# A three-layer kernel: NSA compression with the sequence stationary, and a first norm computed by token

## The reference, cut to what matters

```python
def rms_norm(x, g):
    y = x * rsqrt(mean(x * x, axis=-1, keepdims=True) + 1e-6)
    return y * g

def compress(t, pe, w1, w2):                 # t: B, S, G=4, DH=64; blocks of 32 tokens, stride 16: nc = 31
    pieces = t.reshape(B, S // 16, 16, G, DH)
    blocks = concatenate([pieces[:, i:i + nc] for i in range(2)], axis=2)
    blocks = blocks + pe[None, None, :, None, :]
    flat = blocks.transpose(0, 3, 1, 2, 4).reshape(B, G, nc, 32 * DH)
    return silu(flat @ w1) @ w2              # w1: 2048 x 256, w2: 256 x 64

# layer 1
h = rms_norm(x, pre_norm[0])
q, k, v, glr, z = split(h @ w_in)            # glr: the 16 columns of a low-rank gate
gk = log_sigmoid(glr @ w_gk_up + b_gk) / 16
# layer 2
kc, vc = rope(keys for compression), values for compression
kcmp, vcmp = compress(kc, pe_k, ck_w1, ck_w2), compress(vc, pe_v, cv_w1, cv_w2)
```

## Time and profile before

| | |
|---|---|
| median of three runs | 1395.79 us |
| the profiled execution | 1399.46 us, span 1397.7 us |
| granted TensorE clock over the span | 0.966 of full speed |
| PE busy | 1318.9 us, 94% |
| VectorE busy | 653.3 us, 47% |
| ScalarE busy | 575.2 us, 41% |
| GpSimd busy | 442.8 us, 32% |

### The profile page before, as it was taken

The page is one execution under the profiler, slowest core; times in us unless marked ns, Lnnn a source line. Parts: engine busy times, 40 slices in busy tenths (PEclk is TensorE's granted clock), DMA queues, the critical chain, the costliest instruction groups (busy, mean ns, idle before and its releaser), DMA issues.

```text
span 1397.7 us, 18116 instructions
## 1 busy us (share of the span) xinstructions
PE 1318.9 (94%) x7220; PEld 1027.4 (74%) x7220; DVE 653.3 (47%) x1005; ACT 575.2 (41%) x973; POOL 442.8 (32%) x216
## 2 busy tenths in 40 slices
PE   5999998978799999999988899999999999999997
PEld 2689876846598776656676588787877888888885
DVE  5343135787871654678852513333333283102533
ACT  4244323442333225678864443444444411434332
POOL 4244411442346221110013442222222264444440
PEclk8899999989899999999999999999999999999999
DMA  5222201533456420210002132222222132333211
GB/s 173 70 91 90 91 31 33 178 103 117 137 169 121 84 60 9 61 31 2 2 6 85 37 93 82 60 61 61 61 61 61 31 120 91 91 106 104 90 61 61
DMA packets 129627, 107.49 MB, mean 77 GB/s; under 512 B 36098, under 2 KB 127360, under 8 KB 129552
## 3 DMA queue, kind: packets, MB, share of 16 engines
q1 hardware_dynamic: 129552, 106.44, 26.2%
HBM read 104.33 MB, written 2.10 MB: 76 GB/s over the span
## 4 chain that ended last, share of the span: by engine, by line
PE 87%; DVE 9%; ACT 2%; issue 1%; DMA 1%; SPq 0%; POOL 0%; DVEq 0%; ACTq 0%
PE banks L1021 46%; PE banks L1012 8%; PE banks L988 4%; PE banks L1476 3%; PE banks L1333 3%; PE banks L1367 2%; PE banks L1352 2%; PE banks L1441 2%; PE banks L1222 2%; PE banks L1390 2%; PE banks L1490 1%; DVE act_lo L1566 1%; DVE y_t L1689 1%; PE banks L1204 1%; DVE ada_sum L1663 1%; PE banks L1336 1%
## 5 line engine op out<-in xcount | busy, mean ns | idle before, releaser
L504 POOL TENSOR_TENSOR w_lo<-raw,w_hi 128x1024 fp32r<-128x1024 f32 x170 | 418.1, 2481 | 893.8 <-ACT w_hi L584 893.7
L1021 PE MATMUL banks<-act_hi,w_hi 128*128 128x512 f32 x848 | 336.8, 397 | 5.1 <-DVEq L1728 5.1
L1021 PE MATMUL banks<-act_lo,w_hi 128*128 128x512 f32 x848 | 332.2, 392 | 0.0
L1021 PE MATMUL banks<-act_hi,w_lo 128*128 128x512 f32 x848 | 332.1, 392 | 0.0
L584 ACT ACTIVATE w_hi<-raw 128x1024 fp32r<-128x1024 f32 x170 | 170.1, 1051 | 129.8 <-PE banks L1021 92.2
L1021 PEld LDWEIGHTS banks<-act_hi,w_hi 128*128 128x128 f32 x848 | 160.5, 189 | 41.8 <-DVEq L1728 5.6
L1021 PEld LDWEIGHTS banks<-act_hi,w_lo 128*128 128x128 f32 x848 | 160.5, 189 | 34.1 <-issue 1.4
L1021 PEld LDWEIGHTS banks<-act_lo,w_hi 128*128 128x128 f32 x848 | 160.3, 189 | 34.0
L1012 PE MATMUL banks<-w_hi,act_hi 128*128 128x256 f32 x320 | 91.6, 286 | 0.0
L1012 PE MATMUL banks<-w_hi,act_lo 128*128 128x256 f32 x320 | 91.3, 285 | 0.0
L1012 PE MATMUL banks<-w_lo,act_hi 128*128 128x256 f32 x320 | 91.2, 285 | 0.0
(11 more groups left out here) (324 smaller groups left out, 2194.7 us busy)
## 6 DMA issues: line engine op xcount, KB each, us to landing
raw<-w_in SPq DMA_DIRECT2D x32, 1024.0 KB, 5.7
raw<-gla_w_in SPq DMA_DIRECT2D x13, 1024.0 KB, 5.3
ada_raw<-w_ada SPq DMA_DIRECT2D x8, 1024.0 KB, 5.6
raw<-nsa_w_in SPq DMA_DIRECT2D x32, 256.0 KB, 4.5
raw<-nsa_w_in SPq DMA_DIRECT2D x7, 1024.0 KB, 5.5
raw<-gla_w_out SPq DMA_DIRECT2D x4, 1024.0 KB, 5.1
ada_first<-w_ada SPq DMA_DIRECT2D x4, 1024.0 KB, 7.9
raw<-nsa_w_out SPq DMA_DIRECT2D x16, 256.0 KB, 4.5
```

The lines of the kernel that those rows point to most:

```text
L504: pool.tensor_tensor(w_lo[:, u, k], raw[:, u, k], w_hi[:, u, k].bitcast(F32), ALU.subtract).then_inc(lo_done, 1)
L1021: mm = pe.matmul(b[:], w[:, u, k, m * P:(m + 1) * P], x[:, k, :], start=(k == 0 and n == 0), stop=(k == KT - 1 and n == 2))
```

## The change

In the start, ACT squares x as it landed, by token, each 128 x 512 half of a token tile with its sum over the row (`tok_squares`), and PE makes the sum for all partitions with eight products of a broadcast column and the identity. DVE takes both parts of chunk 0 and the low part of chunk 1 from ACT and POOL. PE interleaves the tiles: three products of chunk 0, then the four of chunk 1 that need no `w_lo`; the eight tiles' `w_lo` products of chunk 1 follow. The gate product moves between the halves of chunk 2.

In the compression, `kv_hi` and `kv_lo` are laid out by half of the block (`part`), group, block and position pair, and are the stationary operand (128 group-block columns, elements 32 bytes apart); the weights move, 256 columns. There is one loop over the 8 tiles, with `between` behind it. The 32nd block of the last group, unused otherwise, holds the positional vectors. ACT copies the result to `hid_raw` (tokens' blocks on the partitions), and PE turns it with `spread`, the identity with a last row of ones added, which also adds the last row, the bias, to all others. ACT then takes the SiLU without a bias. This turning product stands inside chunk 23 for the keys and behind chunk 27 for the values.

```diff
@@ the start: GpSimd
-            split_range(0, C_KC + 1)
+            pool.wait_ge(lo_done, 2 * C_Q + 2)
+            split_range(C_Q + 1, C_KC + 1)
@@ the start: VectorE
+            def first_low(u, part):
+                k = slice(KT // 2 * part, KT // 2 * (part + 1))
+                dve.tensor_tensor(w_lo[:, u, k], raw[:, u, k], w_hi[:, u, k].bitcast(F32), ALU.subtract).then_inc(lo_done, 1)
+            dve.wait_ge(raw_landed[0], 16)
+            for part in range(2):
+                k = slice(KT // 2 * part, KT // 2 * (part + 1))
+                link(dve.tensor_copy(w_hi[:, 0, k], raw[:, 0, k]))
+            dve.sem_inc(hi_done, 2)
+            first_low(0, 0)
             inverse_root(0)
             split_act(0, lambda k: dve.scalar_tensor_tensor(tmp[:, k % 2], xT[:, k], vcol("pre0", k), rstd[:],
-                                                            ALU.mult, ALU.mult))
+                                                            ALU.mult, ALU.mult), after_first=lambda: first_low(0, 1))
+            dve.wait_ge(hi_done, 2 * C_Q + 2)
+            for part in range(2):
+                first_low(C_Q, part)
@@ the start: ScalarE
+            ln_and_exp()
+            for half in range(2):
+                act.wait_ge(x_landed[half], 16)
+                for t in range(TT):
+                    act.activation(qk[:, TT * half + t], x_tok[:, t, half * S:(half + 1) * S], ACT.Square,
+                                   accum_out=tok_squares[:, half, t:t + 1]).then_inc(sq_ready, 1)
             act.wait_ge(consts_ready, 1)
-            norm_front(0)
-            split_high(0, 0, 0, first=True)
             root(0)
-            split_high(1, 0, 1, first=True)
+            split_high(C_Q, 0, C_Q, first=True)
             high_parts(0)
@@ the start: TensorE
-            mean_square(0, ring_squares(0))
+            for half in range(2):
+                for t in range(TT):
+                    pe.wait_ge(sq_ready, TT * half + t + 1)
+                    pe.matmul(bank[4][:, t * P:(t + 1) * P], tok_squares[:, half, t:t + 1].broadcast_to([P, P]), ident[:],
+                              start=(half == 0 and t == 0), stop=(half == 1), skip_group_check=True).then_inc(sq_used, 1)
...
+                if k % (KT // 2) == 0:
+                    pe.wait_ge(hi_done, 2 * C_Q + 2 * k // KT + 1)
+                for m in range(2):
+                    for x in (act_hi, act_lo):
+                        pe.matmul(bank[2 + m][:], w_hi[:, 1, k, m * P:(m + 1) * P], x[:, k, :],
+                                  start=(k == 0 and x is act_hi), stop=False)
+            for k in range(KT):
+                weights_ready(C_Q, k)
+                for m in range(2):
+                    mm = pe.matmul(bank[2 + m][:], w_lo[:, 1, k, m * P:(m + 1) * P], act_hi[:, k, :],
+                                   start=False, stop=(k == KT - 1))
...
+            product(C_Q + 1, (C_Q + 1) // 2, (C_Q + 1) % 2, between=low_rank_up)
@@ the compression: TensorE
-                for m in range(2):
-                    for k in range(KT):
-                        at = 2 * (KT * part + k)
-                        if m == 0:
-                            weights_ready(c, k)
-                        for n, (w, x) in enumerate(((w_hi, kv_hi), (w_lo, kv_hi), (w_hi, kv_lo))):
-                            mm = pe.matmul(bank[6 + m][:, 0:(NG + 1) * NCP].rearrange("p (g c) -> p g c", c=NCP),
-                                           w[:, u, k, m * P:(m + 1) * P],
-                                           x[:, :, at:at + CS * (NCP - 1) + 1:CS],
...
-                    if m == 0 and between is not None:
-                        between()
+                for k in range(KT):
+                    weights_ready(c, k)
+                    for n, (x, w) in enumerate(((kv_hi, w_hi), (kv_hi, w_lo), (kv_lo, w_hi))):
+                        mm = pe.matmul(bank[6][:, 0:CW], x[:, part, :, :, k].rearrange("p g c -> p (g c)"), w[:, u, k, :],
+                                       start=(part == 0 and k == 0 and n == 0), stop=(part == 1 and k == KT - 1 and n == 2))
+                if between is not None:
+                    between()
                 mm.then_inc(bank_full[2 * u + 1], 1)
...
+            def turn_hidden(i):
+                pe.wait_ge(hid_raw_ready, i + 1)
+                for m in range(2):
+                    mm = pe.matmul(bank[7][:, m * P:(m + 1) * P], hid_raw[:, m * P:(m + 1) * P], spread[:], start=True, stop=True)
+                mm.then_inc(hid_turned, 1)
...
-            product(C_VS, C_VS // 2, C_VS % 2, by_tokens=True)
+            product(C_VS, C_VS // 2, C_VS % 2, by_tokens=True, between=lambda: turn_hidden(0))
@@ the compression: ScalarE and VectorE
+        kv_hi = sb("kv_hi", [P, 2, NG, NCP, CS // 2], F32R)
+        def kv_even(part):
+            return kv_full[:, :, CS * part:CS * part + S:2]
...
-                act.activation(kv_hi[:, 0:NG], kv_full[:], ACT.Copy)
-                act.activation(kv_hi[:, NG, 0:CB:2], pe_t[:, i], ACT.Copy).then_inc(kv_hi_done, 1)
+                for part in range(2):
+                    last = act.activation(kv_hi[:, part].rearrange("p g c k -> p g (c k)"), kv_even(part), ACT.Copy)
+                link(last)
+                act.activation(kv_hi[:, :, NG - 1, NCP - 1, :], pe_halves(i), ACT.Copy).then_inc(kv_hi_done, 1)
+            def hidden_raw(i):
+                c = (C_CK, C_CV)[i] + 1
+                act.wait_ge(bank_full[2 * (c % 2) + 1], c // 2 + 1)
+                act.activation(hid_raw[:], bank[6][:, 0:CW], ACT.Copy).then_inc(hid_raw_ready, 1)
             def hidden(i):
-                act.wait_ge(hid_bias_ready, i + 1)
+                act.wait_ge(hid_turned, i + 1)
...
-            hidden_bias(0)
...
-            hidden_bias(1)
```

More of the change, by code:

```diff
@@ L542, in _ @@
             pool.tensor_copy(maskb[:], wide_zero)
-            pool.memset(kv_hi[:, NG].bitcast(F32), 0.0)
-            link(pool.memset(kv_lo[:, NG].bitcast(F32), 0.0))
+            link(pool.affine_select(out=spread[:], in_=ones[:], compare_op=ALU.is_ge, fill=0.0, base=1 - P,
+                                    pattern=[[0, P]], channel_multiplier=1))
+            link(pool.tensor_tensor(spread[:], spread[:], ident[:], ALU.add))
             pool.sem_inc(consts2_ready, 1)
@@ L781, in _ @@
                 untaken(c)
+            hidden_raw(1)
+            untaken(C_GL)
             hidden(1)
-            untaken(C_GL)
             u = C_GL % 2
@@ L1086, in _, with low_rank_up @@
                                    start=(k == 0 and n == 0), stop=(k == KT - 1 and n == 2))
-            mm.then_inc(bank_full[1], 1)
-            pe.sem_inc(bank_full[0], 1)
-            stream(C_Q, 1)
-            pe.wait_ge(bank_free[1], 1)
-            pe.wait_ge(up_landed, 16)
-            pe.wait_ge(rstd_ready, 1)
-            for h in range(GH):
-                pe.matmul(bank[4 + h][:], w_up[:, h * P:(h + 1) * P], glr_t[:], start=True, stop=True).then_inc(up_full, 1)
-            stream(C_Q + 1, 1)
+                if k == KT - 1:
+                    mm.then_inc(bank_full[1], 1)
+                    pe.sem_inc(bank_full[0], 1)
+                if k % (KT // 2) == 0:
[9 more added lines that the diff above has]
+                                   start=False, stop=(k == KT - 1))
+                    if k == KT - 1:
+                        mm.then_inc(bank_full[2 + m], 1)
+            def low_rank_up():
+                pe.wait_ge(bank_free[1], 1)
+                pe.wait_ge(up_landed, 16)
+                pe.wait_ge(rstd_ready, 1)
+                for h in range(GH):
+                    pe.matmul(bank[4 + h][:], w_up[:, h * P:(h + 1) * P], glr_t[:], start=True, stop=True).then_inc(up_full, 1)
+            product(C_Q + 1, (C_Q + 1) // 2, (C_Q + 1) % 2, between=low_rank_up)
             stream(C_K, 2)
@@ L1262, in _ @@
             pe.sem_inc(bank_full[2 * u], 1)
+            turn_hidden(1)
             product(C_NQ, C_NQ // 2, C_NQ % 2)
-            pe.wait_ge(hid_ready, 4)
+            pe.wait_ge(hid_ready, 2)
             for g in range(NG):
@@ L1557, in inverse_root, with split_act @@
                 dve.wait_ge(rstd_ready, n + 1)
-            def split_act(n, scale, to=(act_hi, act_lo), shift=None):
+            def split_act(n, scale, to=(act_hi, act_lo), shift=None, after_first=None):
                 hi, lo = to
@@ L1575, in split_act @@
                     scale(k).then_inc(scaled, 1)
+                    if k == 0 and after_first is not None:
+                        after_first()
                     if k:
@@ L1736, in kv_low @@
                 dve.wait_ge(kv_hi_done, i + 1)
-                dve.tensor_tensor(kv_lo[:, 0:NG], kv_full[:], kv_hi[:, 0:NG].bitcast(F32), ALU.subtract)
-                dve.tensor_tensor(kv_lo[:, NG, 0:CB:2], pe_t[:, i], kv_hi[:, NG, 0:CB:2].bitcast(F32),
-                                  ALU.subtract).then_inc(kv_split, 1)
-            def hidden_bias(i):
-                for m in range(2):
```

(10 more changed lines are left out.)

44 lines of the change are left out of this document (22 added, 22 removed).

## The result

| | before | changed |
|---|---|---|
| median of four runs | 1395.05 us (1391.54 to 1396.73) | 1374.85 us (1371.67 to 1375.83) |
| profiled execution, span | 1399.46, 1397.7 us | 1375.83, 1374.1 us |
| granted clock over the span | 0.966 | 0.971 |

A forecast was written before the change was run, and what follows sets the result against it. TensorE was taken to hold most of the chain, but not to bound the start. Start 13.0 plus compression 7.9 took 20.9 off 1399.5, giving 1378.6; less 3.7 for the median, 1375.0 us; range 1370 to 1379, with rivals 1367 to 1383.

The forecast's parts named there:

- The start, 13.0 us: Start of the kernel: earlier root, faster tiles and interleaved products end chunk 1 at 39.0 instead of 52.1, saving 13.0 us.
- The gate product, 4.62 us: Between the halves of chunk 2: the gate product keeps its 4.62 us and the slow spell behind it.
- The collision, 4.3 us: NSA stage: chunk 23's early split puts two POOL subtractions on DVE's sums, delaying the rotation; 4.3 us lost.
- The pitch, 0.125 us: Compression: products with 256 columns start 0.125 us apart, the spaced weight load just hidden under them.
- the second rival: Compression: the spaced weight load isn't hidden, 0.24 us per product; 13.9 us saved in all, 1381.9 us; chance 0.17.
- Then POOL bounds: Late NSA stage, behind chunk 24: POOL's low halves set the pace, with short PE waits in chunks 26 and 27.
- 7.9 us for the compression: NSA stage: the query product starts at 429.5 instead of 437.4, start gain left out; 7.9 us saved.
- the 3.7 us taken off for the median: Whole kernel: the runs' median, 1395.8, lies 3.7 us below the profiled 1399.5, so 1378.6 became 1375.0.
- The first: NSA stage: chunk 23's early split misses DVE's sums, so 4.3 us are not lost; 25.2 saved, 1370.6 us; chance 0.20.
- The third: Compression: far dearer spaced weight load, break-even at 0.435 us per product; at 0.55, 8.3 us lost, 1404; chance 0.03.
- The fourth: Start: chunk 1 lands late or PE's clock stays low to 35 us; 16.4 us saved in all, 1379.4; chance 0.10.

The follow-up runs named there:

- delayed split: Changed kernel, but ScalarE makes chunk 23's high part only when the third rotation's products are done; 1371.15 us, ratio 0.9848 to the kernel before.
- neighbouring: Changed kernel, but kv_hi and kv_lo laid out so that stationary elements are 4 bytes apart, not 32; 1368.75 us, ratio 0.9842 to the kernel before.
- 8 bytes: Changed kernel, but two neighbouring tiles lie side by side, so stationary elements are 8 bytes apart, not 32; one run, 1371.76 us.
- new order: Changed kernel, but VectorE takes the window keys' rotation behind the fifth piece of weighted sums, not the sixth; 1368.27 us, ratio 0.9826 to the kernel before.
- gate product first: Changed kernel, but the gate product stands ahead of chunk 2, not between its halves; 1375.46 us, ratio 0.9887 to the kernel before.

## Why the prediction was right, and where it was not

**The start, 13.0 us: right.** Chunk 1 ended at 39.07 for a forecast 39.0. Inside it the sums took 2.06 us (2.2), the root ended at 17.0 (16.8), the first product came at 20.3 (20.1), and the low spell ended at 25.0, 4.7 us behind the first product (5.5).

**The gate product, 4.62 us "followed by the same slow spell": wrong by 1.6 us.** It took 3.63, and the distance grew to 14.6. The same 1.6 us came in the kernel with the compression alone, where the gate product kept its old place and 3.63 us too, so the runs give no ground to book them to the change. They are a low spell that fell later and was shorter. What decides where it falls stays open.

**The collision, 4.3 us: right.** 3.9 in two comparisons (compression alone; changed kernel against the delayed split). What the text didn't see is how narrow it is: in two kernels (neighbouring, 8 bytes) the last sum began 1.0 and 0.2 us ahead of GpSimd's pair, and the loss was gone.

**The pitch, 0.125 us: the step that failed.** I set the load's price by the old moving operand, 0.90 ns per element. The load's record is 335 to 340 ns for 128 elements, 2.6 ns each (1.9 from start to start, 0.244/128), and the pitch was the 0.24 that the second rival had. "Then POOL bounds" fell with it: at that pitch TensorE was the slower and waited for no low part of chunks 26 and 27. Of the 7.9 us for the compression 4.3 came in the trace, and by the ratio. The rival's own sum for it, 1.0 us, was too low: it kept 7.13 us for the gates, 0.56 us for the turning product (0.44), and too slow a pace for the keys' second chunk.

**Why the total fits all the same.** 13.0 + 7.9 was forecast. Measured, by the ledger: 13.0 + 1.6 at the start, -2.0 up to the turned keys, +4.2 for the compression with its collision, +1.5 for the spell absent from the second token product: 18.3 at the first query product. The 5.3 us behind it in the profiled executions are mostly (3.8) the trace before being unlucky at 570 us; the 3.7 us taken off for the median may stand for the same luck. So the error of 3.7 us in the compression was made up, between the two profiled executions, by spells of low clock (1.6 and 1.5 gained, 2.0 lost) and by what lies behind the query product; 2.7 us are left over (23.6 for 20.9). The spells the forecast had copied from the trace before as if they belonged to the code. That the time came out right is luck as far as the compression goes, and no proof of the working.

**Rivals.** The first (split misses VectorE) was wrong for this kernel and came true in two variants. The second had the mechanism right (its sum gives 14.0 us, where it says 13.9). The third needed 0.435 us per product, which no spacing up to 32 bytes gave. The fourth's low clock ended at 25.0, not at 35.

## What to carry to other kernels

Before a tile becomes the stationary operand, look at how far apart its elements lie: two neighbours per 16 bytes loaded in 0.19 us here, one in 0.33 to 0.34, which put the starts of products with 256 moving columns 0.24 us apart in place of 0.12; more moving columns were not tried. Read a stall's owner in program order too: moving one block of sums behind the operations that TensorE waited for brought as much at the query product (4.7 us) as halving the pitch did (4.6). And forecast spells of low clock as a spread of 1 to 1.5 us each, not as part of a stage's length.

## What was not expected of the hardware

- The step in the weight load's time between 8 and 16 bytes (0.19 and 0.33 us), with nothing more at 32 (0.34).
- VectorE's rotation operations, which read a bank and one table, took 0.68 us in the middle of GpSimd's run, while the sums with two operands in on-chip memory took 2.46. In the new order's trace:

```profile
351.46 0.68 DVE L1786 SCALAR_TENSOR_TENSOR rope_a<-banks,cosT 128x512 f32<-128x512 f32 x1
```

```profile
346.33 9.75 POOL L515 TENSOR_TENSOR w_lo<-raw,w_hi 128x1024 fp32r<-128x1024 f32 x4 [13.05 <-ACT w_hi L597]
```

- The Trainium skill (SBUF — State Buffer, section "Who interferes with whom") says just this, one operand against two.
- The 96 products of the second token product took 13.2 us, with a low spell, in six traces (before, each part alone, neighbouring elements, 8 bytes, gate product first) and 11.7 in six others. What TensorE did from the third rotation on was alike, instruction for instruction, in the kernel with the compression alone (13.20) and the changed one (11.70).
